# The last stage of a hybrid SSM and mixture-of-experts layer: residual tiles asked for one by one as gathered rows arrive, norm rows loaded first

## The reference

```python
def layer_norm(x, g, b):
    xf = x.astype(jnp.float32)
    mu = jnp.mean(xf, -1, keepdims=True)
    var = jnp.mean(jnp.square(xf - mu), -1, keepdims=True)
    return ((xf - mu) * lax.rsqrt(var + LN_EPS) * g + b).astype(x.dtype)

def reference(x, c, ...):
    cs = jax.nn.silu(c)
    mod = cs @ w_ada[0] + b_ada[0]
    sh1, sc1, g1, sh2, sc2, g2 = jnp.split(mod, 6, axis=-1)
    hm = x * (1.0 + sc1[:, None]) + sh1[:, None]
    y = mamba2_mixer(hm, ...)
    x = layer_norm(DEEPNORM_ALPHA * x + (1.0 + g1[:, None]) * y, ln_g[0, 0], ln_b[0, 0])
    hm = x * (1.0 + sc2[:, None]) + sh2[:, None]
    y = grouped_moe(hm, w_router, b_router, moe_w_gate[0], moe_w_up[0], moe_w_down[0])
    x = layer_norm(DEEPNORM_ALPHA * x + (1.0 + g2[:, None]) * y, ln_g[0, 1], ln_b[0, 1])
    return x
```

## Time and profile before

| | |
|---|---|
| median of three executions | 3032.44 us |
| the profiled execution, whole time | 3034.32 us |
| its span, first to last instruction | 3032.6 us |
| start of the last stage's first load (SP) | 2916.56 us |
| start of its last DVE instruction | 3025.58 us |
| DMA of the program | 610.13 MB, mean 201 GB/s |

### The profile page before, as it was taken

One profiled execution on the slowest core, in us unless ns is written; L12 is line 12 of the kernel. 1 busy time (PEld: TensorE's weight loads), 2 busy tenths in 40 slices (PEclk: granted clock), 3 DMA queues, 4 the chain that ended last, 5 costly groups with the idle time before them and its releaser, 6 DMA issues. The chain is left out here.

```text
span 3032.6 us, 41036 instructions
## 1 busy us (share of the span) xinstructions
PE 2721.6 (90%) x14619; PEld 2316.0 (76%) x14619; DVE 2214.5 (73%) x2649; ACT 1315.3 (43%) x1653; POOL 1480.9 (49%) x753
## 2 busy tenths in 40 slices
PE   3799999999999999999958999869999999999920
PEld 2588888988888888888847888757888888888820
DVE  6578777787878778787744333558888888888857
ACT  4534333333433333243331111115777677777733
POOL 0033333343333343434312222126899999999963
PEclk9899999999999999999979999968999999999965
DMA  7744535345554544455152333139887778677666
GB/s 242 282 180 164 212 132 212 149 145 193 195 177 150 202 170 147 184 181 195 54 185 95 107 114 107 69 133 339 320 303 285 292 260 321 234 281 274 253 261 252
DMA packets 253185, 610.13 MB, mean 201 GB/s; under 512 B 15968, under 2 KB 98560, under 8 KB 244864
## 3 DMA queue, kind: packets, MB, share of 16 engines
q1 hardware_dynamic: 228208, 525.26, 48.1%
q0 software_dynamic: 11520, 41.95, 3.6%
q10 hardware_dynamic: 13328, 41.21, 3.4%
HBM read 600.75 MB, written 99.89 MB: 231 GB/s over the span
## 5 line engine op out<-in xcount | busy, mean ns | idle before, releaser
L1667 DVE TENSOR_TENSOR piece_lo<-piece_raw,piece_hi 128x2048 fp32r<-128x2048 f32 x187 | 563.4, 3031 | 104.0 <-ACT piece_hi L1774 103.9
L1774 ACT CAST piece_hi<-piece_raw 128x2048 fp32r<-128x2048 f32 x280 | 526.5, 1909 | 214.3 <-issue 78.3
L431 PE MATMUL pj<-hm,w_hi 128*128 128x512 f32 x2048 | 536.1, 407 | 46.2 <-DVE hm L951 46.2
L1667 POOL TENSOR_TENSOR piece_lo<-piece_raw,piece_hi 128x2048 fp32r<-128x2048 f32 x93 | 560.0, 6022 | 34.7 <-ACT piece_hi L1774 32.5
L848 DVE SCALAR_TENSOR_TENSOR cv<-ub,par,cv 128x512 f32<-128x512 f32 x384 | 381.1, 992 | 158.3 <-ACT cv L645 149.0
L431 PEld LDWEIGHTS pj<-hm,w_hi 128*128 128x128 f32 x2048 | 380.9, 191 | 120.9 <-DVE hm L951 46.2
L390 POOL TENSOR_TENSOR xw<-xw,t 128x512 f32<-128x512 f32 x64 | 96.7, 1511 | 488.2 <-DVE t L914 488.2
L446 PE MATMUL pz<-wz_hi,hm 128*128 128x256 f32 x2048 | 295.2, 289 | 0.9 <-DVE wz_lo L826 0.3
L446 PEld LDWEIGHTS pz<-wz_hi,hm 128*128 128x128 f32 x2048 | 265.0, 191 | 7.4 <-DVE wz_lo L826 3.7
L371 POOL TENSOR_TENSOR xdt<-xw,tab 128x512 f32<-128x512 f32 x64 | 69.4, 1084 | 398.1 <-ACT xw L664 372.2
L431 PE MATMUL pj<-hm,w_lo 128*128 128x512 f32 x1024 | 254.8, 391 | 0.0
(11 more groups left out here) (308 smaller groups left out, 5783.1 us busy)
## 6 DMA issues: line engine op xcount, KB each, us to landing
hm<-hm_parts SPq DMA_DIRECT2D x30, 4096.0 KB, 13.1
piece_raw<-in_w_gate SPq DMA_DIRECT2D x94, 1024.0 KB
piece_raw<-in_w_up SPq DMA_DIRECT2D x94, 1024.0 KB
piece_raw<-in_w_down SPq DMA_DIRECT2D x92, 1024.0 KB
decay<-acum_rows SPq DMA_DIRECT2D x32, 1024.0 KB, 4.7
w_raw<-in_w_in SPq DMA_DIRECT2D x48, 512.0 KB
expert_out<-ye ACTq DMA_DIRECT2D x46, 512.0 KB
expert_out<-zero_rows SPq DMA_DIRECT2D x8, 2048.0 KB, 19.1
```

Source lines behind the costliest of these rows:

```text
L431: mm = nc.tensor.matmul(pj[m % 2][:], wp[m][:, kk, :], hm[b][:, hp, kk, :], start=q == 0, stop=q == 3 * KK - 1)
L1667: v.tensor_tensor(lo[q][:], raw[q][:], hi[q][:].bitcast(F32), ALU.subtract).then_inc(lo_done[q], 1)
L1774: nc.scalar.copy(hi[q][:], raw[q][:]).then_inc(hi_done[q], 1)
```

## The change

SP's first part is written anew. It asks for `xa` 0, then for the two norm rows, and then for `xa` 1 to 7, each only after the gathered `ya` of the tile ahead has landed. The turns that follow (store a finished tile, load `xa` of tile i + 8) are as before, and so is every other engine.

```diff
-            for i in range(R):
+            load(0)
+            for row, src in ((lng, k.d["ln_g"][1]), (lnb, k.d["ln_b"][1])):
+                sp.dma_start(row[:], src.partition_broadcast(P)).then_inc(row_in, 16)
+            for i in range(1, R):
+                sp.wait_ge(ya_in[i - 1], 16)
                 load(i)
-                if i == 1:
-                    for row, src in ((lng, k.d["ln_g"][1]), (lnb, k.d["ln_b"][1])):
-                        sp.dma_start(row[:], src.partition_broadcast(P)).then_inc(row_in, 16)
             for i in range(TT):
                 sp.wait_ge(o_done, i + 1)
                 sp.dma_start(out[i * P:(i + 1) * P, :], o[i % 2][:]).then_inc(stored[i % 2], 16)
                 if i + R < TT:
                     load(i + R)
```

## The result

The changed kernel takes 3040.03 us in the median of 12 runs, the kernel before 3033.39 us in 12 runs beside them. The ratio is 1.0021, with a 95% interval of 1.0012 to 1.003: slower by 0.21%, 6.4 us, where +5.3 us was forecast. The medians lie 6.6 us apart, and 3040.03 us is 2.3 us over the forecast of 3037.7, inside its range. The profiled execution took 3041.3 us with a span of 3039.5 us.

A forecast was written before the change was run, and what follows sets the result against it. The last stage was taken as bound first by data moving at full DMA rate, after 2990 us by DVE alone. Terms 0 + 0 + 8.5 - 3.2 = +5.3 us on the 3032.44 us median gave 3037.7 us, range 3033.0 to 3041.5.

The forecast's parts named there:

- The early start: Stage start: first gathers release DVE 2.7 us earlier, but `finished(0)` still waits for `rstd(0)` behind 16 gather issues; 0 us.
- The moved rows and later `xa` loads: SP's first loads: norm rows come earlier, `xa` 1 to 7 later but inside the wait for `rstd(0)`; cost 0.
- Store 0 behind the seventh wait: SP's stream: store 0 leaves only after `xa` 7, which waits for gather `ya` 6; issued near 2946.3 us, 6 us late.
- The count of 21 tiles: DMA queues: 21 tiles, 11.0 MB, must have moved before `ya` 6 lands, which gives 2945.6 us.
- `xa` 7 ahead of store 0: SP's queue: `xa` 7 adds 2.54 us to store 0's 6.7; `normed(2)` moves to 2955.5 us, +8.5 us.
- case of the upper bound: SP's queue: `xa` 6 too is still ahead of store 0; `normed(2)` at 2958.0 us, +11.0 us.
- What comes back: Three store waits behind `normed(2)`, 4.3 us in all: three quarters go, 3.2 us, bounds 0 and 4.3.
- The backlog arithmetic: DMA queues at `normed(2)`: 2.7 MB waiting instead of 6.2, then 385 GB/s added against 413 movable, so most later store waits go.
- nothing comes back: Rival for the store waits after `normed(2)`: a burst on SP's queue keeps them alive; +8.5 us, 3040.9 us; chance 0.22.
- rival in which the lost time comes back: `normed(2)` is 6.4 us late, all 4.3 us of later store waits go; about +1.7 us, 3034.1 us; chance 0.25.
- the faster one: Rival: `ya` 6 lands before tile 0 is finished, so store 0 isn't held; -3.9 us, 3028.5 us; chance 0.05.
- the first rival: Same as the rival in which the lost time comes back: after `normed(2)`, later store waits go; 3034.1 us; chance 0.25.

The follow-up runs named there:

- change_rstd0_early: The changed kernel with GpSimd issuing the gathers of six tiles instead of eight ahead of `rstd(0)`: ratio to before 1.0023, stage 116.9 us.
- rows_first: Against the changed kernel, the waits dropped, norm rows still right behind `xa` 0: ratio to before 1.0007, stage 110.7 us.
- half_waits: The changed kernel with `xa` i waiting for `ya` (i - 1) // 2 instead of `ya` i - 1: ratio to before 1.0007, stage 112.6 us.
- change_stores_on_act: The changed kernel with stores issued by ScalarE instead of SP, which keeps the paced loads: ratio to before 1.0009, stage 113.8 us.

## Why the prediction was right

- **The early start, worth 0.** Right. The first `experts_summed` came at 10.8 us into the stage instead of 12.1, 1.3 us earlier (2.7 were forecast), `rstd(0)` at 2937.50, and DVE's wait for it grew from 2.6 to 3.8 us, not to 5. The half of the gain that the first `ya` was to bring didn't come: it released ScalarE 9.4 us into the stage, before 9.2. SP's queue was not nearly empty then, since the second norm row landed 7.6 us after its issue at 2916.88:

```profile
2925.43 1.15 ACT L2011 ACTIVATE ya<-ya,gate_a 128x1024 f32<-128x1024 f32 x1 [28.22 <-DMA ya<-expert_out,slot_a]
...
lnb<-in_ln_b SPq DMA_DIRECT2D x1, 512.0 KB, 7.6
```

  The sum didn't feel it, because the term is covered. `change_rstd0_early` shows that `rstd(0)` was the cover: uncovered, the same stage has tile 0 finished 4.9 us earlier.
- **The moved rows and later `xa` loads, worth 0.** Right: `rows_first` is within 0.4 us of before. DVE did wait 0.8 us for `xa` 1, which the prediction had named as a sign of being wrong. The load took 7.4 us to land where 6.7 were assumed, and the wait lies inside that cover, which the prediction had also counted on.
- **Store 0 behind the seventh wait.** Right in kind. It left 7.7 us later in the stage, 6 were forecast. The count of 21 tiles put the last byte of `ya` 6 at 2945.6 us, and the changed kernel's queues agree. From the stage's start to 2945.5 us they had moved:

```profile
q0 software_dynamic: 1858, 6.80, 58.2%
q1 hardware_dynamic: 1141, 4.19, 39.5%
```

  That is 13 gathers and 8 of SP's tiles. `xa` 7 was issued at 2947.14, so the term of 0.7 us for the signal was too small by 0.8, and the stage in this execution had begun 0.6 us earlier.
- **`xa` 7 ahead of store 0.** Right in kind, and in size partly by luck: issue to release 8.9 us, against 6.7 + 2.54 less SP's issue time, 8.8. Not one tile stood ahead but 1.7, `xa` 7 and most of `xa` 6, which landed at 2950.1 us. That is the case of the upper bound, but each tile cost some 1.5 us and not 2.54, and 0.3 of a tile had stood ahead before the change too. `normed(2)` came 9.3 us later on the clock of the span (2956.37 against 2947.05; 8.5 forecast), 9.9 counted from the stage's start.
- **What comes back.** The one mis-sized term of weight: 2.2 us of the three later store waits went (4.3 to 2.1), not 3.2. Three waits stayed, half as long. The backlog arithmetic had the direction: from 2960 to 3000 us the queues moved only 331 to 376 GB/s in each stretch of ten, under the 413 of full queues. But the stores didn't fall towards 2.7 us with that. Store 5 of the changed kernel, issued at 2979.35, still took 6.3 us, longer than DVE's tile of 5.45, and `normed(7)` waited for it:

```profile
2980.00:2990.00 10.00, 0.00 (x0) 0.00 (x0) 8.57 (x13) 2.52 (x4) 5.28 (x5) 0.50 0.96 352
...
DMA to landing us min/median/max: 6.3/6.3/6.3
```

  Such a store leaves at about the same time as the gathers and the load of a later tile, 2.1 MB in all with itself, and that burst is there without any backlog. The stores fell to 2.6 or 2.7 us only from 3000 us on, where no loads and gathers were left. That the burst keeps them near 6 us fits these rows, but no run tests it by itself.
- **The sum.** 9.9 - 2.2 = 7.7 against 7.5 in the stage, and +6.4 us in the runs against the forecast +5.3. The two misses, +1.4 us on `normed(2)` and 1.0 us less coming back, add up in the stage and don't cancel. For this one profile (+7.5) "nothing comes back" (+8.5) is the nearer case, for the runs (+6.4) the forecast is; the profile still speaks against the rival, since 2.2 us did come back. The prediction gave 0.62 to a change within 0.2%, and the ratio is just outside, with an interval that covers both sides.

The rival in which the lost time comes back fell, and so did the faster one, which needed `ya` 6 before 2940 us. What the prediction didn't weigh is that held-back loads stand ahead of store 0 even if SP is free in time; `half_waits` shows it, 3.2 us on store 0. The fit that the first rival took from the Trainium skill, "DMA: Bandwidth & Descriptors", "Anatomy of one DMA", is one of DMAs issued from GpSimd. SP's stores here took 2.6 to 2.7 us on idle queues, half a us under the 3.2 that it gives, and the changed kernel's store 0 took 8.9.

## What to carry to other kernels

Here a wait put into an in-order issuing stream was paid by what stands behind it in that stream, not by the load that it holds: find the first instruction behind the last new wait and ask who needs it. To hold loads back, hold back only as many as are released before the first store is due, and ask for the rest behind the stores; that gave 1.9 us of stage length here, which the runs don't yet tell from nothing. Where a profile shows waits for a store's buffer, try more buffers first: four instead of two were worth 6.6 us of stage length here, clear in the runs (0.9977), more than any order of the loads. And look for a tiny instruction behind a batch of DMA issues: `rstd(0)` hid what the change gained at the stage's start.

## What the runs showed of the hardware

- The same 512 KB store took 2.6 to 2.7 us to land on idle DMA queues, 6.7 to 6.8 us beside a full gather queue, 7.6 us on a queue of its own beside gathers and loads (`change_stores_on_act`), and 8.9 and 9.9 us with 1.7 and 2.4 held-back tiles ahead of it in its queue (the change, `half_waits`). I had expected a queue of its own to help, and it did not bring the store under 6.7 us.
- Between the last byte of `ya` 6 by the volume moved (2945.6) and SP's next issue (2947.14) lay some 1.5 us. That is an estimate: the first number is the time at which 13 tiles of gathers had passed the queue.
- GpSimd issued the gathers one every 1.24 or 1.25 us, so that 16 of them held `rstd(0)` until 21.5 us into the stage in the change (2937.50 - 2916.00).
